# Turning the expert activations on VectorE and ScalarE instead of TensorE, with the norm weight moved into the weight split

## What is computed

```python
def expert_choice_ffn(h, router_w, w_gate, w_up, w_down):
    xf = h.reshape(n, D)                      # h = rmsnorm(x, g): x * rsqrt(mean(x*x) + EPS) * g
    aff = softmax(xf @ router_w)
    gate, idx = lax.top_k(aff.T, cap)         # cap = 64
    xs = xf[idx]                              # (16 experts, 64 rows, 1024)
    hid = silu(xs @ w_gate[e]) * (xs @ w_up[e])       # 1024 -> 2048
    out = (hid @ w_down[e]) * gate            # 2048 -> 1024
    y = zeros.at[idx].add(out)
```

## Time and profile before

| | us |
|---|---|
| median of 3 runs | 1555.31 (1555.13 to 1555.85) |
| span of the profiled execution | 1553.2 |
| TensorE busy | 1543.2 (99%) |
| VectorE busy | 1300.7 (84%) |
| ScalarE busy | 1044.6 (67%) |
| GpSimd busy | 128.8 (8%) |

### The profile page before, as it was taken

One profiled execution on the slowest core, in us unless ns is written; L12 is line 12 of the kernel. 1 busy time (PEld: TensorE's weight loads), 2 busy tenths in 40 slices (PEclk: granted clock), 3 DMA queues, 4 the chain that ended last, 5 costly groups with the idle time before them and its releaser, 6 DMA issues.

```text
span 1553.2 us, 23079 instructions
## 1 busy us (share of the span) xinstructions
PE 1543.2 (99%) x8616; PEld 1249.3 (80%) x8616; DVE 1300.7 (84%) x1365; ACT 1044.6 (67%) x985; POOL 128.8 (8%) x83
## 2 busy tenths in 40 slices
PE   9999999999999999999999999999999999999998
PEld 8888888888863888888888888888888888888886
DVE  7684786685765899989999998999989999998987
ACT  6453555343453777777777777777777777777777
POOL 0000000000011101102011010101101011010003
PEclk9999999999999999999999999999999999999999
DMA  9633447333476999999999999999999999999998
GB/s 342 195 135 114 148 142 279 96 123 116 139 247 241 400 419 386 387 407 368 419 370 400 388 369 418 371 419 369 393 396 367 421 372 415 370 389 402 380 383 341
DMA packets 155559, 498.47 MB, mean 321 GB/s; under 512 B 10096, under 2 KB 35824, under 8 KB 155504
## 3 DMA queue, kind: packets, MB, share of 16 engines
q1 hardware_dynamic: 144624, 461.54, 76.3%
q0 software_dynamic: 8432, 30.94, 6.4%
q10 hardware_dynamic: 2448, 5.25, 1.3%
HBM read 473.57 MB, written 20.97 MB: 318 GB/s over the span
## 4 chain that ended last, share of the span: by engine, by line
PE 98%; DVE 1%; ACT 0%; issue 0%; DMA 0%; POOLq 0%; POOL 0%; DVEq 0%; ACTq 0%
PE ps L1921 81%; PE ps L1969 4%; PE ps L2060 2%; PE ps L1976 2%; PE ps L2377 2%; PE ps L2018 2%; PE ps L2029 1%; PE ps L2226 1%; PE ps L2227 1%; PE ps L2280 1%; PE ps L2520 0%; PE ps L2222 0%; PE ps L2244 0%; PE ps L2308 0%; DMA xh<-u_rows,first_rows_at 0%
## 5 line engine op out<-in xcount | busy, mean ns | idle before, releaser
L1275 DVE TENSOR_TENSOR w_rest<-raw,w_high 128x2048 fp32r<-128x2048 f32 x212 | 508.9, 2411 | 69.6 <-ACT w_high L1152 50.5
L1152 ACT CAST w_high<-raw 128x2048 fp32r<-128x2048 f32 x184 | 352.5, 1916 | 125.1 <-PE ps L1921 125.1
L1921 PE MATMUL ps<-w_high,xt_high 128*128 128x512 f32 x984 | 304.6, 389 | 0.0
L1921 PE MATMUL ps<-w_high,xt_rest 128*128 128x512 f32 x984 | 304.2, 389 | 0.0
L1921 PE MATMUL ps<-w_rest,xt_high 128*128 128x512 f32 x984 | 304.2, 389 | 0.0
L1275 DVE TENSOR_TENSOR w_rest<-early,w_high 128x2048 fp32r<-128x2048 f32 x90 | 205.6, 2297 | 21.6 <-ACT w_high L1152 21.1
L1921 PEld LDWEIGHTS ps<-w_high,xt_high 128*128 128x128 f32 x984 | 184.7, 188 | 39.2 <-issue 0.8
L1921 PEld LDWEIGHTS ps<-w_high,xt_rest 128*128 128x128 f32 x984 | 184.7, 188 | 38.3
L1921 PEld LDWEIGHTS ps<-w_rest,xt_high 128*128 128x128 f32 x984 | 184.7, 188 | 38.3
L1275 DVE TENSOR_TENSOR w_rest<-raw_more,w_high 128x2048 fp32r<-128x2048 f32 x92 | 208.0, 2285 | 6.4 <-ACT w_high L1152 6.0
L1152 ACT CAST w_high<-early 128x2048 fp32r<-128x2048 f32 x90 | 172.4, 1916 | 58.1 <-PE ps L1921 58.1
(11 more groups left out here) (301 smaller groups left out, 2167.6 us busy)
## 6 DMA issues: line engine op xcount, KB each, us to landing
raw<-w_down SPq DMA_DIRECT2D x64, 1024.0 KB, 8.4
raw<-w_gate SPq DMA_DIRECT2D x62, 1024.0 KB, 8.3
raw<-w_up SPq DMA_DIRECT2D x62, 1024.0 KB, 7.9
raw_more<-w_down SPq DMA_DIRECT2D x32, 1024.0 KB
early<-w_down SPq DMA_DIRECT2D x32, 1024.0 KB, 8.4
raw_more<-w_gate SPq DMA_DIRECT2D x31, 1024.0 KB
raw_more<-w_up SPq DMA_DIRECT2D x31, 1024.0 KB
early<-w_gate SPq DMA_DIRECT2D x31, 1024.0 KB, 10.2
```

The costliest lines, as they stand in the source:

```text
L1152: nc.scalar.copy(w_high[:, i % SLOTS, :], src).then_inc(high_done, 1)
L1275: nc.vector.tensor_tensor(w_rest[:, j, :], src, w_high[:, j, :].bitcast(F32), ALU.subtract).then_inc(rest_done, 1)
L1921: done = nc.tensor.matmul(out, lhs, rhs, start=start and part == 0, stop=stop and part == 2)
```

## The change

For experts 1 to 14 (expert 0 and 15 are kept as they were):

- The hidden halves are turned without TensorE. VectorE transposes each half in 32 x 32 blocks (`turn_blocks`); a block then has the right content at the wrong place. ScalarE copies them to place (`moves`), 16 copies per expert, one for each pair of partition groups: 32 partitions x 16 runs of 32 elements from group a to group c. Then it casts the turned half (`moved_high`) and VectorE makes the rest (`moved_rest`). The last 6 moves and these four copies are placed at the start of the next loop turn, around pairs 12 to 15.
- TensorE keeps the transposes of the rows alone (`next_rows_t`), into banks 2 and 3.
- The norm weight: GpSimd no longer multiplies the rows. The weights of gate and up are multiplied by it instead, per partition: ScalarE's cast becomes an activation with a pointer scale, VectorE's subtraction `(raw * g) - high`.
- For that a pair has to hold one 128-row chunk: the host lays gate beside up (`w_gu`) for experts 1 to 15, and a pair is now 1024 columns of gate and 1024 of up of one chunk. `gate_up` takes them in that order.
- Bank order: gate and up of the first half in banks 0, 1 and 2, 3; of the second half in 6, 7 and 0, 1.

```diff
+MOVES = QUARTERS * QUARTERS
+TURN_STEPS = 2 + MOVES
...
+        blocks = arena[:, 0:2, :].rearrange("p i n -> p (i n)")
+        shuffled = arena[:, 2:4, :].rearrange("p i n -> p (i n)")
+        from_blocks = blocks.rearrange("p (m n) -> p m n", n=P)
+        to_chunks = shuffled.rearrange("p (m n) -> p m n", n=P)
...
+        def weight_of(e, i):
+
+            starts = {0: (GU_PAIRS + 2, 2 * GU_PAIRS + 3, 4 * GU_PAIRS), E - 2: (GU_PAIRS,), E - 1: (0,)} if isinstance(e, int) else {}
+            for at in starts[e] if isinstance(e, int) else (GU_PAIRS, 2 * GU_PAIRS + 1, 4 * GU_PAIRS):
+                if at <= i < at + GU_PAIRS:
+                    return gf_col[:, i - at:i - at + 1]
+            return None
...
             def gate_up_rows(e, h, jj):
+                rows_ = w_gu[bass.ds((2 * (e - 1) + h) * D + jj * P, P), :]
+                return rows_.rearrange("(k p) n -> p k n", p=P)
...
-                pool.wait_ge(gathered, 16 * (e + 2))
-                nc.gpsimd.tensor_tensor(xg, xg, grow[:, :], ALU.mult).then_inc(rows_scaled, 1)
...
+            def moves(e, lo, hi):
+
+                if lo == 0:
+                    act.wait_ge(turn_step, TURN_STEPS * (e - 1) + 2)
+                    act.wait_ge(htr_done, 2 * e)
+                for n in range(lo, hi):
+                    a, c = n % QUARTERS, n // QUARTERS
+                    tokens, columns = slice(a * QUARTER, (a + 1) * QUARTER), slice(c * QUARTER, (c + 1) * QUARTER)
+                    nc.scalar.copy(to_chunks[columns, :, tokens], from_blocks[tokens, :, columns]).then_inc(turn_step, 1)
+
+            def moved_high(e, h):
+                act.wait_ge(turn_step, TURN_STEPS * e)
+                nc.scalar.copy(ht[h][0][:, :], shuffled[:, h * HALF:(h + 1) * HALF]).then_inc(hth_done, 1)
+
...
-                    nc.scalar.copy(w_high[:, i % SLOTS, :], src).then_inc(high_done, 1)
+                    weight = weight_of(e, i)
+                    if weight is None:
+                        nc.scalar.copy(w_high[:, i % SLOTS, :], src).then_inc(high_done, 1)
+                    else:
+                        nc.scalar.activation(w_high[:, i % SLOTS, :], src, ACT.Copy, scale=weight).then_inc(high_done, 1)
...
+            def last_moves(e):
+
+                highs(e, 12, 13)
+                moves(e, 10, 13)
+                highs(e, 13, 14)
+                moves(e, 13, MOVES)
+                highs(e, 14, 15)
+                moved_high(e, 0)
+                highs(e, 15, 16)
+                moved_high(e, 1)
+
             with act.Fori(1, E - 2) as f:
-                highs(f, 12, 19)
+                last_moves(f)
+                highs(f, 16, 19)
                 step_silu(2 * f + 2, pairs_before(f) + 16, 0)
                 highs(f, 19, 28)
-                step_silu(2 * f + 3, pairs_before(f) + 25, 1)
-                highs(f, 28, 31)
-                rows_high(f + 2)
+                step_silu(2 * f + 3, pairs_before(f) + 25, 1, 6)
+                highs(f, 28, 30)
+                moves(f + 1, 0, 2)
+                highs(f, 30, 31)
+                rows_high(f + 2, 2)
                 highs(f, 31, 32)
-                hidden_high(2 * f + 2, 0, 2)
-                highs(f, 32, 36)
-                hidden_high(2 * f + 3, 1, 6, pairs_before(f) + 32)
+                moves(f + 1, 2, 4)
+                highs(f, 32, 33)
+                moves(f + 1, 4, 6)
+                highs(f, 33, 34)
+                moves(f + 1, 6, 8)
+                highs(f, 34, 35)
+                moves(f + 1, 8, 10)
+                highs(f, 35, 36)
                 result(f, pairs_before(f) + 32)
...
+                    nc.vector.scalar_tensor_tensor(out=w_rest[:, j, :], in0=src, scalar=weight, in1=w_high[:, j, :].bitcast(F32),
+                                                   op0=ALU.mult, op1=ALU.subtract).then_inc(rest_done, 1)
...
+            def turn_blocks(e, h):
+
+                if h == 0 and not (isinstance(e, int) and e == 1):
+                    dve.wait_ge(turn_step, TURN_STEPS * (e - 1))
+                dve.wait_ge(hid_done, 2 * e + h + 1)
+                nc.vector.transpose(blocks[:, h * HALF:(h + 1) * HALF], acts[h]).then_inc(turn_step, 1)
+
+            def moved_rest(e, h):
+                dve.wait_ge(hth_done, 2 * e + h + 1)
+                nc.vector.tensor_tensor(ht[h][1][:, :], shuffled[:, h * HALF:(h + 1) * HALF], ht[h][0][:, :].bitcast(F32), ALU.subtract).then_inc(htr_done, 1)
+
...
+            def moved_rests(e):
+
+                rests(e, 12, 15)
+                moved_rest(e, 0)
+                rests(e, 15, 16)
+                moved_rest(e, 1)
+
             with dve.Fori(1, E - 2) as f:
-                rests(f, 12, 19)
+                moved_rests(f)
+                rests(f, 16, 19)
                 step_hidden(2 * f + 2, 0)
+                turn_blocks(f + 1, 0)
                 rests(f, 19, 28)
-                step_hidden(2 * f + 3, 1)
+                step_hidden(2 * f + 3, 1, 0)
+                turn_blocks(f + 1, 1)
                 rests(f, 28, 31)
-                rows_rest(f + 2)
-                rests(f, 31, 32)
-                hidden_rest(2 * f + 2, 0, 2)
-                rests(f, 32, 36)
-                hidden_rest(2 * f + 3, 1)
+                rows_rest(f + 2, 2)
+                rests(f, 31, 36)
...
+            def gate_up(e, lo, gate_bank, up_bank, rows_done, gate_free=None, up_free=None):
+
+                pe.wait_ge(xtr_done, rows_done)
+                if gate_free is not None:
+                    pe.wait_ge(*gate_free)
+                for kc in range(KC):
+                    j, at = (lo + kc) % SLOTS, slice(kc * P, (kc + 1) * P)
+                    pe.wait_ge(rest_done, SLOTS * body_q(e, lo + kc) + j + 1)
+                    for what, bank_ in enumerate((gate_bank, up_bank)):
+                        if what and kc == 0 and up_free is not None:
+                            pe.wait_ge(*up_free)
+                        last = products([(bank(bank_ + n), xt_high[:, at], xt_rest[:, at], *w(j, what * HALF + n * BANK, BANK),
                                           kc == 0, kc == KC - 1) for n in range(2)])
...
-            def all_turns(e):
-
-                pe.wait_ge(rows_scaled, e + 1)
-                pe.wait_ge(hid_done, 2 * e + 2)
-                pe.wait_ge(htr_done, 2 * e)
+            def next_rows_t(e):
+
+                pe.wait_ge(gathered, 16 * (e + 2))
+                pe.wait_ge(hid_done, 2 * e + 1)
                 if not isinstance(e, int):
                     pe.nop(nofuse=True)
-                rows_t(0)
-                hidden_t(acts[0], 2)
-                hidden_t(acts[1], 6)
+                rows_t(2)
...
             with pe.Fori(1, E - 2) as f:
-                gate_up(f, 8, (xtr_done, f + 3), (htr_done, 2 * f + 1))
+                gate_up(f, 8, 0, 2, f + 3, (hid_done, 2 * f + 2))
                 pe.wait_ge(ys_done, f + 1)
                 down(2 * f, 0, f, 16, 0, 1)
-                gate_up(f, 17, (silu_done, 2 * f + 3), (hid_done, 2 * f + 3))
+                gate_up(f, 17, 6, 0, f + 3, None, (silu_done, 2 * f + 3))
                 down(2 * f, 0, f, 24, 1, 4)
-                all_turns(f + 1)
+                next_rows_t(f + 1)
                 down(2 * f + 1, 1, f, 28)
```

More of the change, by code:

```diff
@@ L395, in encoder_kernel @@
         third_silu_done, third_hid_done = sem("third_silu_done"), sem("third_hid_done")
-        half_silu, half_hid = sem("half_silu"), sem("half_hid")
+        half_silu = sem("half_silu")
+        gate_used = sem("gate_used")
         first_xt_done = sem("first_xt_done")
@@ L497, in load_first @@
                 if i < SLOTS:
-                    return load(FRONT_Q, i, gate_up_rows(0, 0, i))
+                    return load(FRONT_Q, i, first_gate_up_rows(0, i))
                 if i < SLOTS + 2:
@@ L1102, in _, with step_silu @@
                     cast_qk(b + 1, 0, "q", 1)
-            def step_silu(s, used_by_gate_up, odd=0):
-                act.wait_ge(pair_used, used_by_gate_up)
+            def step_silu(s, used_by_gate_up, odd=0, gate_bank=0, used=None):
+                act.wait_ge(used or pair_used, used_by_gate_up)
                 if isinstance(s, int) and s == 0:
@@ L1189, in _ @@
             highs(0, 21, 30)
-            step_silu(3, pairs_before(0) + 27, 1)
-            highs(0, 30, 33)
-            rows_high(2)
+            step_silu(3, pairs_before(0) + 27, 1, 6)
+            highs(0, 30, 32)
+            moves(1, 0, 2)
+            highs(0, 32, 33)
+            rows_high(2, 2)
             highs(0, 33, 34)
-            hidden_high(2, 0, 2)
-            highs(0, 34, 36)
-            hidden_high(3, 1, 6, pairs_before(0) + 32)
+            moves(1, 2, 5)
+            highs(0, 34, 35)
+            moves(1, 5, 8)
+            highs(0, 35, 36)
             result(0, pairs_before(0) + 32)
+            moves(1, 8, 10)
+            def last_moves(e):
[7 more added lines that the diff above has]
+                moved_high(e, 1)
```

(50 more changed lines are left out.)

42 lines of the change are left out of this document (22 added, 20 removed).

## The result

| | before | after |
|---|---|---|
| median, us | 1555.22 | 1606.86 (1606.47 to 1606.97) |
| span of the profiled execution, us | 1553.2 | 1604.6 |

The change makes the kernel slower: the ratio is 1.0332 (95% interval 1.0317 to 1.0347), 51.6 us. The forecast was 1602, the range 1563 to 1620.

What follows compares the result with a forecast made beforehand. TensorE bounded the kernel before (98% of the chain); after the change a loop of 70.6 us per expert sets the pace. That adds 47 us to the 1553.2 span, plus 2.1 outside it: 1602 us, range 1563 to 1620.

Steps and rivals of the forecast that it cites:

- The bound and its floor: TensorE, experts 1 to 14: 32 of 48 transposes go, so its floor per expert falls from 67.14 to 66.05 us.
- The prices: Per-instruction costs on ScalarE and VectorE: moves 0.64 us apart, weighted splits 2.02 long, rests 2.34, block transpose 1.13 plus 0.12.
- three odd places of the trace before: ScalarE copies whose start partition differs from the previous copy's; none overlaps, hence 0.64 us per move.
- rival 2: VectorE's block transpose takes 2.3 us; one stands in the loop, adding 14 us, for 1616 us; chance 0.14.
- The two rules: ScalarE copies: unconditional 93 ns overlap gives 0.52 us per move; waiting after a start-quadrant change, stated for VectorE, supports the forecast.
- The costs set at nothing: Per expert, off the path: ScalarE +1.7 us, VectorE -2.1 and +1.0; loads and bank order also cost 0.
- The loop: From TensorE's pair 27 to the next, through ScalarE, VectorE and TensorE: 70.6 us per expert, above 66.05.
- the pairs named: TensorE stalls ahead of pairs 13 to 16 and 19, 4.5 us per expert.
- +3.45: Extra us per expert, 70.6 against 67.14; +48 us over 14 experts, less 1.2 for the last.
- The restarts of TensorE: Longer first products after each TensorE wait, not priced: five stops at 0.12 would add 8 us, within the upper end.
- 3.7 us of slack: How far ScalarE and VectorE together may fall behind before TensorE stops, since split i needs pair i-4 used.

Runs made afterwards that it cites:

- the kernel with the even half: Kernel before, with only the even hidden half turned by VectorE and ScalarE, two short moves behind each of eight splits: 1548.2 us, ratio 0.9955.

## Why the prediction was right, step by step

**The bound and its floor.** 66.05 us was worked out for TensorE alone; without the moves it stands at 66.15.

**The prices.** Moves 0.618 us long and about 0.64 apart, as taken from three odd places of the trace before. Weighted splits 2.01 (forecast 2.02), three-operand rests 2.35 (2.34). The transpose, which no row showed, takes 1.25 us: the low end of its bounds, so rival 2 falls. The two rules that the prediction took from the Trainium skill part ways here, and the measurement decides. The overlap that the Trainium skill (ScalarE: Activation LUTs, What ACT_TABLE_LOAD costs) gives without a condition is seen here only where both start partitions stay the same. That is the held rule of the Trainium skill (VectorE: DVE Perf Modes, Two Vector instructions with no wait between them), which is said of VectorE; the experiments show it for ScalarE, in 1570.8 against 1606.9 us.

**The costs set at nothing.** GpSimd's product, the layout, the bank order, the weighted split beside TensorE's pace: the run with them alone is at 1.0001. Two of their sizes were a little off, where it costs nothing: ScalarE's +1.7 us per expert measured +1.4, and VectorE's -2.1 + 1.0 measured -0.75. Loads land in

```profile
DMA to landing us min/median/max: 5.9/7.5/9.0
```

(answers to the earlier trace rows), a little sooner than before.

**The loop.** 70.6 forecast, 70.76 measured; stops ahead of exactly the pairs named. Its terms can be read off the timelines above, from start to start: transposes 0.76 us (925.24 to 926.00), ScalarE 26.97 (to 952.97), VectorE 18.31 (to 971.28), TensorE 24.7 (to the next transposes); forecast were 0.63, 27.0, 18.3 and 24.7. That it is a loop through three engines, and not one busy engine, is shown by what leaving out or shortening its terms did: 2.6 us less per expert with the overlaps back (2.7 forecast), 1.0 with plain splits and rests (1.0 to 1.1).

**What was off: 4.6 us** of 51.6. TensorE's transpose runs after the change, the first and the last of the 14 turned experts:

```profile
575.22 0.71 PE L2460 MATMUL ps<-ident,xh 64*128 64x64 f32 x16
...
642.15 0.71 PE L2460 MATMUL ps<-ident,xh 64*128 64x64 f32 x16
...
1491.29 0.71 PE L2460 MATMUL ps<-ident,xh 64*128 64x64 f32 x16
...
1539.32 0.71 PE L2460 MATMUL ps<-ident,xh 64*128 64x64 f32 x16
```

The first takes 66.93 us where it took 61.73 before: +5.2 instead of the +3.45 that I had counted for each, with six stops and not five. In expert 0 part of the moves stand in groups of three instead of two, which is the likely cause; it wasn't tried. The twelve between 642.15 and 1491.29 take 70.76 each, 0.16 over the sum; the last costs 2.65 (48.03 against 45.38 before) instead of 2.25. Together that is 4.1 us; the rest is rounding, and 0.2 by which the medians differ more than the spans. The restarts of TensorE, for which the range allowed 8 us, add nothing that shows: only the one ahead of pair 19 stands in the loop, in a term that came out as forecast, and the other four come while ScalarE and VectorE set the pace. The prediction said that it did not price them, and not why they would be small; that part was luck.

## What to carry to other kernels

Work taken off the busiest engine is a gain only if what replaces it fits where the other engines have room: count the work that comes in one piece between two fixed points (the lump) against the slack of the buffers, and don't go by busy shares. Follow the chain around once through all engines (here four weight slots = 3.7 us of slack) and compare it with the bound's own period. Take the price of many small copies from rows with the same change of partitions, not from the same shape; and put such copies where the engine already waits.

## What the runs showed of the hardware that I had not expected

That the hold (a copy starts only at the end of the one before) works on ScalarE was in three rows before; that a change of either the first input partition or the first output partition is enough, was new (1601.3 and 1602.6 us with one side fixed, 1570.8 with both). In the kernel with the turn alone GpSimd's 128x1024 product takes 3.8 us instead of the 2.5 of the earlier trace rows (3.4 at 913.97 in the kernel with the even half); whether it waits for a rest to end there, no run tells apart. After the change GpSimd's gather instruction shows 2.28 us in the mean, where the mean was 1.46 before (11 of them between 700 and 1500 us each):

```profile
L757 POOL DMA_INDIRECT xh<-u_rows,rows x11 | 25.1, 2284 | 561.6 <-PE ps L2460 561.6
```

It goes with the turn taken off TensorE, and not with the moves or the weights: over the whole span its mean is 1.45 us with the weights alone and 2.16 without the moves. Why is open; it isn't on the critical path here.
